# Experts' weights in packets of 8192 bytes: two successive rows of a matrix in one partition

## The reference, cut to what matters

```python
def modulate(h, shift, scale):
    return h * (1.0 + scale[:, None, :]) + shift[:, None, :]
...
    hu = lax.ragged_dot(xs, w1, sizes)
    h_gate, h_up = jnp.split(hu, 2, axis=-1)
    ys = lax.ragged_dot(jax.nn.silu(h_gate) * h_up, w2, sizes)
    ys = ys * flat_gate[order][:, None].astype(ys.dtype)
    out = jnp.zeros_like(t).at[tok_s].add(ys)
...
        h = modulate(rms_norm(x, norm2_g[l]), sh2, sc2)
        y = hier_moe(h, w_router_group[l], b_router_group[l], w_router_expert[l],
                     b_router_expert[l], w_expert_in[l], w_expert_out[l])
        x = x + g2[:, None, :] * y
```

## Time and profile before

| | |
|---|---|
| median of 3 runs (range) | 2311.27 us (2306.36 to 2318.2) |
| profiled execution, its own time | 2302.7 us |
| profiled execution, span | 2300.9 us, mean granted clock 0.972 |
| TensorE busy with matmuls | 2134.7 us, 93% |
| VectorE, ScalarE, GpSimd busy | 963.1, 685.9, 284.1 us |
| moved by DMA | 657.30 MB in 242742 packets |
| experts' stage, layer 0 | 336.6 to 822.9 us of the span |
| experts' stage, layer 1 | 1125.0 to 1619.8 us of the span |

### The profile page before, as it was taken

One profiled execution on the slowest core, in us unless ns is written; L12 is line 12 of the kernel. 1 busy time (PEld: TensorE's weight loads), 2 busy tenths in 40 slices (PEclk: granted clock), 3 DMA queues, 4 the chain that ended last, 5 costly groups with the idle time before them and its releaser, 6 DMA issues.

```text
span 2300.9 us, 30193 instructions
## 1 busy us (share of the span) xinstructions
PE 2134.7 (93%) x12867; PEld 1500.7 (65%) x12867; DVE 963.1 (42%) x1892; ACT 685.9 (30%) x1224; POOL 284.1 (12%) x145
## 2 busy tenths in 40 slices
PE   6999888999999989998899999999998899998998
PEld 4787674555544567777645555554774699978997
DVE  2466632212111136566312221221245577756776
ACT  3434421101101034353211110110203555555554
POOL 4554420000000034554000000000000000000000
PEclk8999989999999989999899999999999999998999
DMA  9965669999999976657689999999355375334651
GB/s 347 325 226 206 242 241 380 409 409 409 409 409 409 408 275 224 220 220 293 271 347 389 409 409 409 409 409 404 126 206 213 130 235 187 109 115 167 199 173 48
DMA packets 242742, 657.30 MB, mean 286 GB/s; under 512 B 12923, under 2 KB 116837, under 8 KB 230184
## 3 DMA queue, kind: packets, MB, share of 16 engines
q1 hardware_dynamic: 239936, 651.74, 74.8%
q0 software_dynamic: 1184, 2.08, 0.3%
q10 hardware_dynamic: 1480, 1.45, 0.2%
HBM read 654.17 MB, written 1.06 MB: 285 GB/s over the span
## 4 chain that ended last, share of the span: by engine, by line
PE 86%; DVE 10%; ACT 3%; issue 1%; DMA 0%; POOL 0%; ACTq 0%; DVEq 0%
PE ps L410 85%; DVE AR L1971 2%; DVE AR L747 1%; DVE AR L2018 1%; PE ps L2648 0%; DVE ARr L1646 0%; DVE AR L1231 0%; ACT AR L818 0%; ACT AR L2621 0%; ACT HBr L387 0%; PE ps L2472 0%; DMA hT<-in_onehot 0%; DVE ringr L393 0%; DVE AR L1114 0%; ACT hTr L827 0%
## 5 line engine op out<-in xcount | busy, mean ns | idle before, releaser
L410 PE MATMUL ps<-ring,AR 128*64 128x512 f32 (+2 forms) x2016 | 514.7, 577 | 31.4 <-DVE AR L2018 31.4
L410 PE MATMUL ps<-XLr,HBr 128*128 128x256 f32 x1280 | 375.5, 293 | 22.1 <-DVE ringr L393 6.9
L410 PE MATMUL ps<-AR 128*128 128x128 f32 (+6 forms) x2088 | 380.9, 345 | 14.0 <-DVE AR L1952 7.5
L410 PEld LDWEIGHTS ps<-ring,AR 128*64 128x64 f32 (+1 forms) x2016 | 196.8, 140 | 268.9 <-issue 264.0
L410 PEld LDWEIGHTS ps<-AR 128*128 128x128 f32 (+2 forms) x2088 | 290.0, 192 | 119.5 <-issue 76.4
L410 PE MATMUL ps<-hTr,ringr 128*128 128x256 f32 x1280 | 366.5, 286 | 0.0
L410 PE MATMUL ps<-hTr,HBr 128*128 128x256 f32 x1280 | 366.2, 286 | 0.0
L393 POOL TENSOR_TENSOR ringr<-ring,HBr 128x1024 fp32r<-128x1024 f32 x110 | 266.3, 2436 | 777.6 <-ACT HBr L387 777.4
L387 ACT ACTIVATE HBr<-ring 128x1024 fp32r<-128x1024 f32 x260 | 266.3, 1050 | 196.6 <-PE ps L410 179.9
L410 PEld LDWEIGHTS ps<-XLr,HBr 128*128 128x128 f32 x1280 | 249.4, 195 | 43.6 <-issue 24.8
L410 PEld LDWEIGHTS ps<-hTr,ringr 128*128 128x128 f32 x1280 | 250.2, 195 | 2.1 <-issue 1.0
(11 more groups left out here) (311 smaller groups left out, 2593.9 us busy)
## 6 DMA issues: line engine op xcount, KB each, us to landing
ring<-in_w_expert_in SPq DMA_DIRECT2D x155, 1024.0 KB, 14.8
ring<-in_w_expert_out SPq DMA_DIRECT2D x81, 1024.0 KB, 11.0
ring<-in_mod_w SPq DMA_DIRECT2D x48, 1024.0 KB, 6.6
ring<-in_ffn_w_up SPq DMA_DIRECT2D x44, 1024.0 KB, 5.2
ring<-in_w_in SPq DMA_DIRECT2D x40, 1024.0 KB, 5.6
ring<-in_w_ada SPq DMA_DIRECT2D x40, 1024.0 KB, 8.2
HB<-in_w_expert_in SPq DMA_DIRECT2D x35, 1024.0 KB, 14.6
HB<-in_w_expert_out SPq DMA_DIRECT2D x23, 1024.0 KB, 12.3
```

Source lines behind the costliest of these rows:

```text
L410: return pe.op.matmul(out_, lhsT, rhs, start=start, stop=stop, **kw)
```

## The change

Each piece of 256 rows of an expert's matrix is read so that partition r gets the successive rows 2r and 2r + 1, 8192 bytes in one stretch of memory, in place of rows r and 128 + r. Block k of a piece in its slot is then the even rows (k even) or the odd rows (k odd) of the piece. The activations are dealt out to match: `by_twos` takes each second column of 256, as the stationary operand of the gather, as the operand of the turn's transposes, and in the part for crowded experts. Scale and shift, which hold one value a partition, are dealt out once a layer: eight small matmuls in `pe_router_shift` with each second column of the identity, and one more copy in `dve_router_shift` into `m.cs` (16 columns). ScalarE and VectorE read `m.cs` in place of `m.coef` and `m.shift`, and wait for that copy.

```diff
+            m.cs = small(16)
...
+        def row_pairs(w):
+            return w.rearrange("(p k) f -> p (k f)", k=2).rearrange("p (o f) -> p o f", o=1)
+
+        def by_twos(ap, k, at=0):
+            a = at + k // 2 * 256 + k % 2
+            return ap[:, a:a + 255:2]
+
...
-                            load(sp, (which, l, e, n), by_rows(W[e, n * 256:(n + 1) * 256, :]), 2, 1024, all_)
+                            load(sp, (which, l, e, n), row_pairs(W[e, n * 256:(n + 1) * 256, :]), 1, 2048, all_)
...
-                t = mm(pe, b[:, 0:36], C("ones"), v3(m.wsh, 8)[:, k, :], False, k == 7)
+                mm(pe, b[:, 0:36], C("ones"), v3(m.wsh, 8)[:, k, :], False, k == 7)
+
+            for i, src in enumerate((m.coef, m.shift)):
+                for odd in range(2):
+                    for h in range(2):
+                        t = mm(pe, b[64 * h:64 * h + 64, 64 + 8 * i + 4 * odd:68 + 8 * i + 4 * odd], ident[:, odd:odd + 127:2],
+                               src[:, h:h + 7:2], True, True)
...
-            dve.op.tensor_copy(m.rsh, bank["shift", l][:, 0:36]).then_inc(*dve_moe.inc("shift", l))
+            dve.op.tensor_copy(m.rsh, bank["shift", l][:, 0:36]).then_inc(*dve_moe.inc())
+            dve.op.tensor_copy(m.cs.rearrange("p (i n odd) -> p i odd n", i=2, odd=2),
+                               bank["shift", l][:, 64:80].rearrange("p (i odd n) -> p i odd n", i=2, odd=2)).then_inc(*dve_moe.inc("shift", l))
...
-                        a = j * 1024 + (4 * k4 + k) * 128
-                        t = mm(pe, b[:, k * 128:(k + 1) * 128], m.xtok[:, a:a + 128], P3[:, j, :], j == 0, j == 1)
+                        t = mm(pe, b[:, k * 128:(k + 1) * 128], by_twos(m.xtok, 4 * k4 + k, j * 1024), P3[:, j, :], j == 0, j == 1)
...
+            act.wait_ge(*dve_moe["shift", l])
             act.wait_ge(*pe_moe["xg", l, p, 0])
...
-                                  scale=m.coef[:, k:k + 1], bias=m.shift[:, k:k + 1]).then_inc(*act_moe.inc("xg", l, p))
+                                  scale=m.cs[:, k:k + 1], bias=m.cs[:, 8 + k:9 + k]).then_inc(*act_moe.inc("xg", l, p))
...
+            dve.wait_ge(*dve_moe["shift", l])
             dve.wait_ge(*pe_moe["xg", l, p, 1])
...
-                t = pe.op.transpose(bank["turn", l, p][:, k * 128:(k + 1) * 128], m.th["th", l, p][:, k * 128:(k + 1) * 128], ident)
+                t = pe.op.transpose(bank["turn", l, p][:, k * 128:(k + 1) * 128], by_twos(m.th["th", l, p], k), ident)
```

More of the change, by code:

```diff
@@ L1718, in sp_moe @@
                         W, r = (W1, n) if n < 4 else (W2, n - 4)
-                        src = W[bass.ds(e, 1), r * 256:(r + 1) * 256, :].rearrange("o (k p) f -> p (o k) f", p=128)
+                        src = W[bass.ds(e, 1), r * 256:(r + 1) * 256, :].rearrange("o (p k) f -> p (o k) f", p=128)
                         part.op.dma_start(v3(slot_at[2 + n][0], 2), src).then_inc(*q_over[l].inc("w", j, n))
@@ L1970, in dve_gather @@
                 c = slice((k - 4) * 128, (k - 3) * 128)
-                dve.op.tensor_scalar(m.x["x", l, p][:, k * 128:(k + 1) * 128], bank["xg", l, p, 1][:, c], m.coef[:, k:k + 1],
-                                     m.shift[:, k:k + 1], ALU.mult, ALU.add).then_inc(*dve_moe.inc("xg", l, p))
+                dve.op.tensor_scalar(m.x["x", l, p][:, k * 128:(k + 1) * 128], bank["xg", l, p, 1][:, c], m.cs[:, k:k + 1],
+                                     m.cs[:, 8 + k:9 + k], ALU.mult, ALU.add).then_inc(*dve_moe.inc("xg", l, p))
         def pe_up(pe, l, m, p):
@@ L2179, in dve_over_all @@
                 for k in range(8):
-                    dve.op.tensor_scalar(xv[:, k * 64:(k + 1) * 64], ps[0][:, k * 64:(k + 1) * 64], m.coef[:, k:k + 1],
-                                         m.shift[:, k:k + 1], ALU.mult, ALU.add).then_inc(*D_.inc("xg", j))
+                    dve.op.tensor_scalar(xv[:, k * 64:(k + 1) * 64], ps[0][:, k * 64:(k + 1) * 64], m.cs[:, k:k + 1],
+                                         m.cs[:, 8 + k:9 + k], ALU.mult, ALU.add).then_inc(*D_.inc("xg", j))
                 dve.wait_ge(*act_over[l]["th", j])
@@ L2210, in pe_over_all @@
                     for t_ in range(2):
-                        mm(pe, ps[0][:, k * 64:(k + 1) * 64], m.xtok[:, t_ * 1024 + k * 128:t_ * 1024 + (k + 1) * 128],
-                           P3[:, t_, 0:64], t_ == 0, t_ == 1)
+                        mm(pe, ps[0][:, k * 64:(k + 1) * 64], by_twos(m.xtok, k, t_ * 1024), P3[:, t_, 0:64], t_ == 0, t_ == 1)
                 for t_ in range(2):
@@ L2223, in pe_over_all @@
                 for k in range(4):
-                    t = pe.op.transpose(ps[0][:, k * 64:(k + 1) * 64], tv[0:64, k * 128:(k + 1) * 128], ident[0:64, 0:64])
+                    t = pe.op.transpose(ps[0][:, k * 64:(k + 1) * 64], by_twos(tv[0:64, :], k), ident[0:64, 0:64])
                 t.then_inc(*pe_over[l].inc("turn", j))
```

## The result

The changed kernel takes 2320.13 us, the median of 18 runs (2316.47 to 2332.51), beside 2312.71 for 18 runs of the kernel before (2306.36 to 2318.2). The ratio is 1.0044, with a 95% interval of 1.0034 to 1.0054. The first interval makes the kernel slower by 8 to 12 us, 0.3 to 0.5%, and the two medians differ by 7.4 us; the forecast was 2314.

The account below looks back on a forecast made before the run. TensorE and its handovers were taken as the bound, the DMA 1.5% behind. The shift's 2.9 us, with 0 for loads, gather and turn, on the median 2311.3 gave 2314 us; own range 2305 to 2320, wide range 2300 to 2332.

Parts of the forecast that it names:

- The bound: Experts' stages: TensorE and its handovers set the 30.30 us period of a pair; the DMA is second, 1.5% behind.
- The loads: Experts' loads: 8192-byte packets, near 193,600 in all, stage rate 415 GB/s, landing some 12 us, nothing saved on the path.
- the DMA gets slower: Rival, experts' loads: 8192-byte stretches out of one piece move slower, at 390 GB/s 28 us more, 2342 us; chance 0.05.
- the packets don't change: Rival, experts' loads: 8192-byte stretches are cut in two, rate and landing stay, forecast's time; counted within the forecast's 0.73.
- its queue was a hidden bound: Rival: earlier landing shortens stage ends and first pairs, 10 us or a little over, 2301 to 2304; over 0.5%, chance 0.05.
- The gap behind layer 1's last scatter: After layer 1's experts: a shorter DMA queue could give back up to 4.9 us; taken as 0, kept for the range.
- The gather's operand: Gather's 32 records a pair: strided weight loads have no slack; taken as nothing, at most 110 ns more a record.
- The turn: The turn's four transposes read each second column: nothing, or at most 0.44 us a pair, 14 us in 32.
- The shift: Router's shift: 16 added TensorE records on the path, 0.9 to 2.0 us, taken as 1.4 a layer, 2.9 for both.
- The sum: Whole kernel: profiled execution 2302.7 + 2.9 - 0 = 2305.6 us; as a median 2311.3 + 2.9 = 2314 us.
- the bound of 0.5%: What a measurement can tell from no change, 11.6 us; chances: same 0.73, slower 0.21, faster 0.06.
- the wide range: Whole kernel: 2300 to 2332 us, past the transposes' case, leaving out about 2 in 10.

Follow-up runs that it names:

- the loads alone: Kernel before with only the experts' loads changed to 8192-byte packets, activations not dealt out: 2312.65 us, ratio 1.0002.
- dealt version: The change with ScalarE dealing out the gather's operand as it copies it, and the small products moved into the router's idle time: 2313.78 us, 1.0005.
- the products alone: Kernel before with the eight small products and VectorE's copy added in the router's shift, result unused: 2318.16 us, ratio 1.0021.
- the second measurement: The changed kernel run once more beside the kernel before, for a second profile: ratio 1.006 (1.0036 to 1.0083).
- loads and strides: The changed kernel without the eight small products and their copy, old coefficients kept: 2311.46 us, ratio 0.9995 to the kernel before.
- moving the products: The changed kernel with the eight products moved from the shift to TensorE's idle time behind the turned context tokens: 2321.78 us, 1.0041 to before.

## Why the prediction came out as it did

**The bound** was read rightly. No load stands in the chain of after, and the loads alone give a ratio of 1.0002 and a period of 30.31 us, at 414 GB/s from 380 to 500 us.

**The loads** behaved as said: packets 193,591 for "near 193,600", a rate of 411 to 418 for 415. At the end of layer 0's stage (764 to 796 us) a load into the ring lands after

```profile
ring<-in_w_expert_in SPq DMA_DIRECT2D x3, 1024.0 KB, 14.8
```

where it was 20.3; I said near 12, and early in the stage it is 9.8. The rivals that the DMA gets slower and that the packets don't change are excluded by these rows. That its queue was a hidden bound worth 10 us is excluded by the loads alone, which win at most 2.5 us by their interval. The gap behind layer 1's last scatter stayed as well, "issue" of 1.92 us for 1.65, so the 4.9 us that I kept for it were not there to be had.

**The gather's operand** is the step that was mis-sized. I took nothing; the term is 5.9 ns a record, 0.19 us a pair, 6.1 us in all (4.8 ± 0.9 at an equal clock). The reasoning on slack was right: 4 ns more on a weight load went into the path at once. The reason for taking nothing, that a column 8 bytes on is still one read, does not hold to the ns, and the lower bound, one read however far, fails at 16 bytes. The dealt version shows it from the other side: with the gather's operand contiguous again the piece is back at 28.06 us, and the kernel is 8.0 us faster than the one that differs from it in this and in ScalarE's copies alone (6.0 at an equal clock).

**The turn** costs 0.04 us in its own records. The dealt version keeps its step, and has a period of 30.31 us: nothing, as forecast.

**The shift** was forecast at 1.4 us a layer and took 2.22. Its records cost less than the lower bound, 0.57 for 0.9, and the fall of the clock behind them costs 1.65, a term that the sum did not have. The run of 10.22 us comes in both profiles of the change and with the products alone, and goes in the three kernels without products at that place, so the products there cause it. Alone they cost 1.0021 or 2 to 7 us, for 4.4 in the rows.

**The sum.** 6.1 + 4.4 = 10.5 us of bills against my 2.9. That puts the forecast 7.6 too low, and the median came out 6.1 above it. The total is inside the bound of 0.5% and the wide range, though the second measurement's 1.006 lies just over that bound, and 2320.13 just outside the forecast's own range, 2305 to 2320. It held because the two missed terms are small, not because they were foreseen. By the sign that the prediction gave itself, that it is wrong if the piece of 28.06 grows, it was wrong in this part: the piece is 28.25, though the period of 31 or 34 us that it named for strided loads did not come. The scatter, which I put at 5 us to either side, goes mostly with the mean granted clock.

**What stays open** is why strided operands without the small products have a mean clock of 0.971 to 0.972, worth 5 to 7 us against the 0.968 of before, and with them do not; by medians the products, added to loads and strides, carry all of the change's loss, 9 us. Open too is why moving the products won only 1.4 us at an equal clock. No run moved the clock's falls on purpose.

No version with the reference's output beat the kernel before; the strided operands alone did by 3 us, with weights and features that don't match. The best with the new layout, the dealt one, takes 2313.78 us: 6 less than the change, and level with before.

## What to carry to other kernels

A layout that eases a resource which no wait in the chain names earns nothing, and what it costs on the engine that does stand there is paid in full: here 4 ns on a weight load with no slack became 6 us. Keep a stationary fp32 operand contiguous, or at most at a step of two elements, and deal out by the copy that writes it. When parts of some tenths of a per cent are measured alone, compare them at an equal granted clock as well as by the plain ratio, because a part that lowers the clock hides its cost in the first, and take a second profile of the same kernel before a stretch that differs is put down to the edit.

## What the runs showed of the hardware

- A load of 128 fp32 stationary columns takes 192, 196, 329 and 335 ns at steps of 4, 8, 16 and 32 bytes.
- Sixteen records of 64 columns by 4 take 36 ns each, and behind them the granted clock fell to the lower level for a few microseconds though TensorE was busy for the whole stretch ahead (2.50 us of 2.50). The run with the products alone shows the same run of 10.22 us. The clock also fell at 32 records of one column in layer 1, to 0.53 in a stretch of 2.5 us without the small products, and to 0.50 in three such stretches in the change.
- Packets of 8192 bytes moved mostly at 413 to 436 GB/s between pauses, those of 4096 bytes at 392 to 416 without a pause.
- In one kernel, executions differ by some 9 us in one stretch of 220 us, and spans go with the mean granted clock by 1.5 us for each 0.001.
